# Linear attention: step table, predicated merge of block levels, a gate chain in two steps

## Chip, core and metric

One Trainium2 chip, of which the kernel uses one core. The time is device microseconds of one execution. Every time below is in microseconds unless it says ns. The engines are named as the profile names them: PE is TensorE's matmul, PEld its weight load, DVE is VectorE, ACT is ScalarE, POOL is GpSimd, SP is SyncE, which issues the weight transfers.

## What is computed

Two blocks in float32 on a sequence of 256 positions with 1024 channels. The first is a hybrid layer (attention with forgetting, a short convolution, a gated delta rule, a gated feed-forward part with a convolution, and a gated embedding `ple`). The second block has two layers; the mixer of its second one is a gated linear attention, the part that most of the change is about:

```python
def _gla_mixer(h, w_in, w_gk_up, b_gk, norm_gain, w_out):
    proj = h @ w_in
    q, k, v, g_out, gk_low = jnp.split(proj, [...], axis=-1)
    log_a = jax.nn.log_sigmoid(gk_low @ w_gk_up + b_gk) / GLA_GATE_TEMP
    ...
    b = jnp.cumsum(gi, axis=2)
    o_inter = jnp.einsum('bhlk,bhkv->bhlv', qi * jnp.exp(b), state)
    diff = b[:, :, :, None, :] - b[:, :, None, :, :]
    decay = jnp.exp(jnp.where(causal[:, :, None], diff, -jnp.inf))
    attn = jnp.einsum('bhijk,bhjk->bhij', qi[:, :, :, None, :] * decay, ki)
    o_intra = jnp.einsum('bhij,bhjv->bhiv', attn, vi)
    ...
    o = _rmsnorm(o, norm_gain) * silu(g_out)
    return o @ w_out
```

There are 4 heads, with 128 key channels and 256 value channels each.

## The kernel before

**Units.** Every large product is cut into units of 1 MB of weights (128 partitions x 2048 columns, float32). SP loads a unit into one of 5 buffers (`raw`, L742) when the unit five before it is done. A float32 product is made of three passes over a high part and a low part: ACT copies the unit rounded to fp32r into `whi` (L865, `split_high`, 3 buffers, so it waits until the unit three before is done), DVE writes the difference into `low` (L1241, `split_low`), and PE multiplies high by high, high by low and low by high (L1874 to L1876 for units of kind C, which fill one bank of PSUM, 4 or 5 in turn; L1891 to L1893 for kind D, which accumulate over four units into banks 0 to 3; L1860 to L1864 for a C unit that starts right behind a normalisation).

**Order.** One list, `order`, is written at build time, and each engine takes from it, in that order, the part it has in every step; each engine works its own instructions strictly in turn and waits on semaphores. `("mm", u, 0)` and `("mm", u, 1)` are the two halves of unit u on PE. At half 0 of unit u ACT makes the high part of unit u + 2, at half 1 DVE makes the low part of unit u + 2. In the front part and in the first mixer of the second block, steps are placed by a table of half units. In linear attention `weave` spreads them by weights: a list of steps, each with an amount of unit halves that goes in front of it.

**Linear attention** has 12 units of `gla_w_in`: four C units for q and k (124 to 127), four D units for v (128 to 131), four C units for the output gate (132 to 135). Then four D units of `gla_w_out` (136 to 139). Between them stand:
- `norm_wide` (PE L1914) spreads the norm's reciprocal over PSUM, and DVE copies it (L1297). `gla_low` (PE L2167 to L2169) makes the gate's 16 channels. `gla_qk` (DVE L1302, `scaled`) takes q and k from PSUM, which frees the C unit's bank.
- the gate chain, `gla_gate`: PE L2176 and L2177, DVE L1730 and L1731, ACT's Exp and Ln (L1130, L1132, each behind a table load), and DVE's subtraction L1733. All of DVE's part is one step, so DVE waits for ACT in the middle of it. `gla_cum` (PE L2186, ACT L1137) sums over positions.
- eight levels of blocks of 1, 2, 4 ... 128 positions. Level l has `gla_arg` (DVE L1770, L1771: exponents), ACT's Exp (L1146), `gla_mul` (DVE L1777, L1778: q and k times it, into one buffer `Cl`), `gla_pairs(l + 1)` (PE L2208: 8 products into banks 6 and 7) and `gla_mask(l + 1)`, which takes them out of PSUM: level 0 by L1750 times the identity into `attn`, levels 1 to 4 by L1750 times a 0/1 matrix `lev` into a second buffer `atmp` and L1752, `attn + atmp`; levels 5 to 8 by copies of blocks (L1745, L1738).
- `gla_values` (PE L2219, L2220), `gla_sum` (ACT's sums of squares L858 and Sqrt L1036, DVE L1252 and L1584), `gla_g` (DVE L1302, ACT's Silu L1158), and `gla_turn` (PE transposes L2233, DVE L1790, ACT L1168, DVE L1797), which makes the input of `gla_w_out`.

**The norm** at the end of each part (`last_product`): the last unit's result is added to x in three pieces (DVE L1632 or L1630), PE transposes x (L1907), ACT takes the high part of each pair of tiles (L896), DVE its low part (L1281, `("norm", i, pair)`), and DVE makes one more unit's low part (`split_late`). Norm 2 is the one in front of `w_ple_gate`, whose first units are 75, 76 and 77.

Of the kernel before, what the change touches and what calls it, by code (L numbers as in the profile page):

```python
# [22 lines left out]
def build(nc, a):  # L23

    T, D = a["x"].shape[1:]
# [460 lines left out]
    fill = []
    for i in range(4):
        u = unit_d(w_gla, 256 * i, "h", 2 * i, i == 0, i == 3, h_ready, c0=2 * GK)
        fill.append((u, ("gla_v", u)) if i == 3 else (u,))
    for e in range(2):  # L490
        u = unit_c(w_gla, 2 * GK + D + 256 * e, "h", h_ready)
        fill.append((u, ("gla_g", e, u)))
    mixed = [(2, ("gla_pairs", 0))]
    for l in range(8):
        fill_by = (1.8, 1.2) if l < 5 else (1, 0.8)
        mixed += [(0, ("gla_arg", l)), (fill_by[0], ("gla_mask", l)), (0, ("gla_mul", l)),
                  (fill_by[1], ("gla_pairs", l + 1))]
    weave(fill, mixed + [(0.5, ("gla_mask", 8))])
    fill = []
    for e in range(2, D // 256):  # L500
        u = unit_c(w_gla, 2 * GK + D + 256 * e, "h", h_ready)
        fill.append((u, ("gla_g", e, u)))
# [1777 lines left out]
```

## Time and profile before

| what | us |
|---|---|
| median of 3 runs | 1202.05 |
| lowest and highest of them | 1201.32, 1202.52 |
| the profiled execution, its own time | 1200.95 |
| span of its instructions | 1199.2 |

The profile is one execution. Its own time is its span and 1.75 us around it. PE is busy in 95% of the span, the other engines in 64% (DVE), 46% (ACT) and 4% (POOL). The chain of work that ended last is 77% PE, 14% DVE and 4% ACT. The section on rows below shows, for two stretches of the span, the timeline (one line for an instruction or a run of like ones) and the waits: a wait is time in which an engine stood idle in front of an instruction, with the instruction that released it. The granted clock is 1.00 at 2.4 GHz and 0.50 at 1.2 GHz.

### The profile page before, as it was taken

What the parts mean: (1) busy time and instruction counts of PE and PEld (TensorE: products, weight loads), DVE (VectorE), ACT (ScalarE), POOL (GpSimd) and SP (SyncE); (2) the same over time, 40 slices, a digit from 0 to 9 for tenths busy, and PEclk for the clock granted to TensorE, in tenths of its full rate; (3) what the DMA queues carried; (4) which work ended last, traced back from release to release, by engine and by line L of the source; (5) the groups of instructions that cost most, each with busy time, mean ns of one, the idle gap of its engine ahead of it and who ended that gap; (6) DMA issues with size and microseconds to landing.
All of it is one profiled execution on the core that took longest, in us unless ns stands there. A gap on an engine that the chain in (4) does not pass through costs nothing.

```text
span 1199.2 us, 17834 instructions
## 1 busy us (share of the span) xinstructions
PE 1139.3 (95%) x7630; PEld 1034.0 (86%) x7630; DVE 772.3 (64%) x918; ACT 550.6 (46%) x637; POOL 45.1 (4%) x108
## 2 busy tenths in 40 slices
PE   6989998999999999999998999999989999999996
PEld 6888887898889999997787799999878888999995
DVE  4585777564467988887677564554566856555554
ACT  5466554223445443345555444444443454444443
POOL 8000000000000000000004100000000000000000
PEclk9998999999999999999999999999999999999999
DMA  7765864355355555554453455655533335556551
GB/s 244 201 160 77 132 144 106 63 115 105 107 185 177 177 183 196 184 179 172 141 186 108 141 177 183 200 180 184 183 125 105 106 105 159 193 176 191 196 175 53
DMA packets 128448, 185.08 MB, mean 154 GB/s; under 512 B 6868, under 2 KB 104161, under 8 KB 128370
## 3 DMA queue, kind: packets, MB, share of 16 engines
q1 hardware_dynamic: 123136, 182.46, 51.6%
q10 hardware_dynamic: 4690, 1.36, 0.5%
q8 instruction: 60, 0.98, 0.3%
q0 software_dynamic: 544, 0.13, 0.1%
q14 instruction: 18, 0.15, 0.0%
HBM read 182.89 MB, written 1.05 MB: 153 GB/s over the span
## 4 chain that ended last, share of the span: by engine, by line
PE 77%; DVE 14%; ACT 4%; issue 3%; DMA 1%; ACTq 0%; SPq 0%; DVEq 0%
PE ps L1874 12%; PE ps L1875 12%; PE ps L1876 12%; PE ps L1891 10%; PE ps L1892 10%; PE ps L1893 10%; DVE low L1241 4%; ACT whi L865 1%; PE ps L2078 1%; PE ps L1907 1%; PE ps L2208 1%; PE ps L2084 1%; PE ps L2087 1%; DMA raw<-in_w_in 1%; DVE hlo L1281 1%
## 5 line engine op out<-in xcount | busy, mean ns | idle before, releaser
L865 ACT ACTIVATE whi<-raw 128x2048 fp32r<-128x2048 f32 x172 | 327.9, 1911 | 348.1 <-PE ps L1876 168.0
L1241 DVE TENSOR_TENSOR low<-raw,whi 128x2048 fp32r<-128x2048 f32 x172 | 393.4, 2289 | 56.9 <-ACT whi L865 54.0
L1874 PE MATMUL ps<-hhi,whi 128*128 128x256 f32 x1424 | 410.0, 288 | 10.4 <-DVE arena L1302 5.0
L1875 PE MATMUL ps<-hlo,whi 128*128 128x256 f32 x1424 | 405.2, 285 | 0.0
L1876 PE MATMUL ps<-hhi,low 128*128 128x256 f32 x1424 | 405.1, 284 | 0.0
L1874 PEld LDWEIGHTS ps<-hhi,whi 128*128 128x128 f32 x1424 | 275.2, 193 | 17.0 <-DVE low L1241 10.2
L1875 PEld LDWEIGHTS ps<-hlo,whi 128*128 128x128 f32 x1424 | 275.2, 193 | 1.7 <-issue 0.2
L1876 PEld LDWEIGHTS ps<-hhi,low 128*128 128x128 f32 x1424 | 275.1, 193 | 0.0
L1891 PE MATMUL ps<-whi,ahi 128*128 128x512 f32 x416 | 164.7, 396 | 8.4 <-issue 4.6
L1892 PE MATMUL ps<-low,ahi 128*128 128x512 f32 x416 | 162.8, 391 | 0.0
L1893 PE MATMUL ps<-whi,alo 128*128 128x512 f32 x416 | 162.5, 391 | 0.0
L1891 PEld LDWEIGHTS ps<-whi,ahi 128*128 128x128 f32 x416 | 78.6, 189 | 25.1 <-issue 8.7
L1893 PEld LDWEIGHTS ps<-whi,alo 128*128 128x128 f32 x416 | 78.4, 188 | 17.0
L1892 PEld LDWEIGHTS ps<-low,ahi 128*128 128x128 f32 x416 | 78.7, 189 | 14.6
L1719 DVE TENSOR_TENSOR cy<-cy 128x512 f32<-128x512 f32 x32 | 22.1, 692 | 75.4 <-ACT cy L1118 75.4
L1724 DVE TENSOR_TENSOR alo<-cy,ahi 128x512 fp32r<-128x512 f32 x32 | 22.2, 692 | 72.8 <-ACT ahi L1126 72.8
L1891 PE MATMUL ps<-whi,hhi 128*128 128x512 f32 x160 | 64.4, 402 | 4.6 <-DVE hlo L1281 2.7
L1892 PE MATMUL ps<-low,hhi 128*128 128x512 f32 x160 | 63.0, 394 | 0.0
L1893 PE MATMUL ps<-whi,hlo 128*128 128x512 f32 x160 | 63.0, 394 | 0.0
L1891 PEld LDWEIGHTS ps<-whi,hhi 128*128 128x128 f32 x160 | 30.4, 190 | 11.5 <-DVE low L1241 5.2
L1408 DVE SCALAR_TENSOR_TENSOR cy<-conv,colp,cy 128x256 f32<-128x256 f32 x88 | 38.8, 482 | 1.6
L1893 PEld LDWEIGHTS ps<-whi,hlo 128*128 128x128 f32 x160 | 30.5, 190 | 6.6
(381 smaller groups left out, 1199.7 us busy)
## 6 DMA issues: line engine op xcount, KB each, us to landing
raw<-in_ffn_w SPq DMA_DIRECT2D x64, 1024.0 KB, 5.2
raw<-in_w_in SPq DMA_DIRECT2D x32, 1024.0 KB, 10.3
raw<-in_w_up SPq DMA_DIRECT2D x22, 1024.0 KB, 5.1
raw<-in_gla_w_in SPq DMA_DIRECT2D x12, 1024.0 KB, 5.2
raw<-in_w_down SPq DMA_DIRECT2D x11, 1024.0 KB, 4.9
raw<-in_ab_w_in SPq DMA_DIRECT2D x8, 1024.0 KB, 5.2
raw<-in_w_branch SPq DMA_DIRECT2D x6, 1024.0 KB, 6.0
raw<-in_w_o SPq DMA_DIRECT2D x4, 1024.0 KB, 4.7
```

Source lines behind the costliest of these rows:

```text
L865: act.activation(whi[:, u % SPLIT, :], raw[:, u % RAW, :], ACT.Copy).then_inc(sem("hi_done"), 1)
L1241: dve.tensor_tensor(wlo[:, u % RAW, :], raw[:, u % RAW, :], whi[:, u % SPLIT, :].bitcast(F32), ALU.subtract).then_inc(sem("lo_done"), 1)
L1281: dve.scalar_tensor_tensor(out=hlo[:, k, :], in0=ps[:, turn_banks[i][pair], (k % 2) * T:(k % 2 + 1) * T], scalar=gain(i, k), in1=hhi[:, k, ...
L1408: ins = dve.scalar_tensor_tensor(out=out[:, q, :], in0=src, scalar=w, in1=out[:, q, :], op0=ALU.mult, op1=ALU.add)
L1719: own(dve.tensor_tensor(y, y, y, ALU.mult), "relu2_sq", i + 1)
L1724: dve.tensor_tensor(alo[:, s, :], cy[:, i % 2, :, :], ahi[:, s, :].bitcast(F32), ALU.subtract)\
L1874: pe.matmul(out, wh, hi[:, k0 + k, :], start=k == 0, stop=False)
L1875: pe.matmul(out, wh, lo[:, k0 + k, :], start=False, stop=False)
L1876: ins = pe.matmul(out, wl, hi[:, k0 + k, :], start=False, stop=k == nk - 1)
L1891: pe.matmul(out, xh, wh, start=start, stop=False)
L1892: pe.matmul(out, xh, wl, start=False, stop=False)
L1893: ins = pe.matmul(out, xl, wh, start=False, stop=stop)
```

## The change

1. In `last_product`, for norm 2 alone, `split_late` moves from behind all four pairs to between pair 1 and pair 2.
2. In linear attention, the units and the steps between them are placed by a table of half units in place of `weave`. D units of v wait for the gate's part of DVE (`gla_abs`) as well.
3. `gla_gate` on DVE is two steps, `gla_gate` and `gla_decay`, with other steps between them.
4. `gla_mask` of levels 1 to 4 is one `copy_predicated` from PSUM into `attn`, under the mask `lev`; `atmp` is gone.
5. The waits of `gla_arg(0)` for q and k move to `gla_mul(0)`; the other `gla_mul` wait until PE has read `Cl` of the level before.

```diff
-        for pair in range(1, 4):
-            step("norm", i, pair)
-        step("split_late", u)
+        step("norm", i, 1)
+        if i == 2:
+            step("split_late", u)
+        step("norm", i, 2)
+        step("norm", i, 3)
+        if i != 2:
+            step("split_late", u)
...
-    weave(fill, [(3, ("norm_wide", 5)), (0, ("gla_low",)), (1, ("gla_gate",)), (4, ("gla_cum",))])
...
+        u = unit_d(w_gla, 256 * i, "h", 2 * i, i == 0, i == 3, h_ready + [("gla_abs", 1)], c0=2 * GK)
...
+    steps_at = {
+        1: [("norm_wide", 5), ("gla_low",)],
+        3: [("gla_gate",)],
...
+        17: [("gla_arg", 6), ("gla_mul", 6), ("gla_mask", 6)],
...
+    for at, (u, *then) in enumerate(linear):
+        order.append(("mm", u, 0))
+        flush()
+        for s in steps_at.get(2 * at, ()):
+            step(*s)
+        order.append(("mm", u, 1))
+        held.extend(then)
+        for s in steps_at.get(2 * at + 1, ()):
+            step(*s)
...
                 dve.scalar_tensor_tensor(out=gla, in0=gmin, scalar=-2.0, in1=two, op0=ALU.mult, op1=ALU.add).then_inc(sem("gla_abs"), 1)
+
+            def gla_decay():
                 dve.wait_ge(sem("gla_ln"), 2)
                 own(dve.tensor_tensor(gla, gmin, gla, ALU.subtract), "gla_la", 1)
...
-                mask = ident[:, :] if l == 0 else lev[:, l - 1, :]
-                dst = attn if l == 0 else atmp
-                own(dve.tensor_tensor(dst, two, wide(mask.unsqueeze(1), [TT * GH, P]), ALU.mult), "gla_took", l + 1)
-                if l:
-                    link(dve.tensor_tensor(attn, attn, atmp, ALU.add))
+                if l == 0:
+                    own(dve.tensor_tensor(attn, two, wide(ident[:, :].unsqueeze(1), [TT * GH, P]), ALU.mult), "gla_took", 1)
+                    return
+                mask = lev[:, l - 1, :].bitcast(mybir.dt.uint32)
+                own(dve.copy_predicated(attn, wide(mask.unsqueeze(1), [TT * GH, P]), two), "gla_took", l + 1)
...
                 if l == 0:
                     dve.wait_ge(sem("gla_b"), 2)
-                    dve.wait_ge(*gla_qk_ready[0])
-                    dve.wait_ge(*gla_qk_ready[1])
...
                 dve.wait_ge(sem("gla_E"), l + 1)
+                if l == 0:
+                    dve.wait_ge(*gla_qk_ready[0])
+                    dve.wait_ge(*gla_qk_ready[1])
+                else:
+                    dve.wait_ge(sem("gla_paired"), 2 * l + 2)
```

How instructions stand in a row, at three places. The line numbers of the changed kernel are other than those of before: its L1669 is L1632 of before, L1318 is L1281, L1278 is L1241, L1326 to L1351 are L1289 to L1314, L1767 and L1768 are L1730 and L1731, L1772 is L1733, L1807 and L1808 are L1770 and L1771, L1788 is L1750, L1819 and L1820 are L1777 and L1778.

**DVE at norm 2.** The rows are the additions to x, the low parts of the norm's tiles (`hlo`) and the low part of unit 76 (`low`). Before:

```order
L1632 TENSOR_TENSOR xres<-xres,ps 128x1024
L1632 TENSOR_TENSOR xres<-xres,ps 128x512
L1281 SCALAR_TENSOR_TENSOR hlo<-ps,colp,hhi 128x256 x2
L1632 TENSOR_TENSOR xres<-xres,ps 128x512
L1281 SCALAR_TENSOR_TENSOR hlo<-ps,colp,hhi 128x256 x6
L1241 TENSOR_TENSOR low<-raw,whi 128x2048
L1289 RECIPROCAL rs<-rs 128x2
```

Changed:

```order
L1669 TENSOR_TENSOR xres<-xres,ps 128x1024
L1669 TENSOR_TENSOR xres<-xres,ps 128x512
L1318 SCALAR_TENSOR_TENSOR hlo<-ps,colp,hhi 128x256 x2
L1669 TENSOR_TENSOR xres<-xres,ps 128x512
L1318 SCALAR_TENSOR_TENSOR hlo<-ps,colp,hhi 128x256 x2
L1278 TENSOR_TENSOR low<-raw,whi 128x2048
L1318 SCALAR_TENSOR_TENSOR hlo<-ps,colp,hhi 128x256 x4
L1326 RECIPROCAL rs<-rs 128x2
```

The low part of unit 76 moved in front of the last four low parts of the norm.

**DVE from the start of linear attention to its first exponents.** `low` rows are units 126, 127, 128 and on; L1302 (L1339) is `gla_qk`; L1730, L1731 and L1733 (L1767, L1768 and L1772) the gate. Before:

```order
L1241 TENSOR_TENSOR low<-raw,whi 128x2048
L1297 COPY arena<-ps 128x256
L1302 SCALAR_TENSOR_TENSOR arena<-ps,arena 128x512
L1314 TENSOR_TENSOR arena<-ps,arena 16x256
L1241 TENSOR_TENSOR low<-raw,whi 128x2048
L1730 TENSOR_SCALAR arena<-ps 128x1024
L1731 SCALAR_TENSOR_TENSOR arena<-arena,ps 128x1024
L1733 TENSOR_TENSOR arena<-arena 128x1024
L1241 TENSOR_TENSOR low<-raw,whi 128x2048
L1302 SCALAR_TENSOR_TENSOR arena<-ps,arena 128x512
L1241 TENSOR_TENSOR low<-raw,whi 128x2048
L1302 SCALAR_TENSOR_TENSOR arena<-ps,arena 128x512 x2
```

Changed:

```order
L1278 TENSOR_TENSOR low<-raw,whi 128x2048
L1334 COPY arena<-ps 128x256
L1351 TENSOR_TENSOR arena<-ps,arena 16x256
L1339 SCALAR_TENSOR_TENSOR arena<-ps,arena 128x512
L1278 TENSOR_TENSOR low<-raw,whi 128x2048
L1767 TENSOR_SCALAR arena<-ps 128x1024
L1768 SCALAR_TENSOR_TENSOR arena<-arena,ps 128x1024
L1339 SCALAR_TENSOR_TENSOR arena<-ps,arena 128x512
L1772 TENSOR_TENSOR arena<-arena 128x1024
L1278 TENSOR_TENSOR low<-raw,whi 128x2048
L1807 TENSOR_TENSOR arena<-arena 128x512
L1808 TENSOR_TENSOR arena<-arena 128x512
```

`gla_qk` of unit 125 moved from behind the gate's subtraction and a low part to in front of both, and the first exponents now come before `gla_qk` of units 126 and 127. On PE, `norm_wide` and `gla_low` moved from behind the first half of unit 125 to in front of it, and `gla_cum` from behind unit 127 to in front of it.

**DVE at levels 0 to 2.** Before:

```order
L1750 TENSOR_TENSOR arena<-ps,ident 128x1024
L1777 TENSOR_TENSOR arena<-arena 128x512
L1778 TENSOR_TENSOR arena<-arena 128x512
L1241 TENSOR_TENSOR low<-raw,whi 128x2048
L1770 TENSOR_TENSOR arena<-arena 128x256x2
L1771 TENSOR_TENSOR arena<-arena 128x256x2
L1750 TENSOR_TENSOR arena<-ps,lev 128x1024
L1752 TENSOR_TENSOR arena<-arena 128x1024
L1777 TENSOR_TENSOR arena<-arena 128x256x2
L1778 TENSOR_TENSOR arena<-arena 128x256x2
```

Changed:

```order
L1788 TENSOR_TENSOR arena<-ps,ident 128x1024
L1819 TENSOR_TENSOR arena<-arena 128x512
L1820 TENSOR_TENSOR arena<-arena 128x512
L1807 TENSOR_TENSOR arena<-arena 128x256x2
L1808 TENSOR_TENSOR arena<-arena 128x256x2
L1278 TENSOR_TENSOR low<-raw,whi 128x2048
L1791 COPY_PREDICATED arena<-lev,ps 128x1024
L1819 TENSOR_TENSOR arena<-arena 128x256x2
L1820 TENSOR_TENSOR arena<-arena 128x256x2
```

The unit's low part moved behind the exponents of level 1, and the pair of instructions that merged a level is one.

## Rows read from the trace of the kernel before

**Rows 1.** The page's first part: busy us, share, instructions of each engine.
```profile
PE 1139.3 (95%) x7630; PEld 1034.0 (86%) x7630; DVE 772.3 (64%) x918; ACT 550.6 (46%) x637; POOL 45.1 (4%) x108
```

**Rows 2.** Waits of PE, 860 to 1000: waiting line, releaser, total, times, longest.
```profile
PE ps L1874 <- DVE arena L1302: 5.0, 1, 5.0
PE ps L2208 <- DVE arena L1778: 4.8, 3, 2.6
PE ps L1891 <- issue: 2.8, 1, 2.8
PE ps L1874 <- DVE low L1241: 0.2, 1, 0.2
```

**Rows 3.** Timeline at norm 2: start, duration, engine, line, idle before it and releaser.
```profile
549.50 1.92 ACT L865 ACTIVATE whi<-raw 128x2048 fp32r<-128x2048 f32 x1
...
561.58 1.66 DVE L1281 SCALAR_TENSOR_TENSOR hlo<-ps,colp,hhi 128x256 fp32r<-128x256 f32 x4 [2.49 <-ACT hhi L896]
...
565.50 0.50 PE L1891 MATMUL ps<-whi,hhi 128*128 128x512 f32 x1 [1.83 <-DVE low L1241]
...
568.01 4.49 DVE L1241 TENSOR_TENSOR low<-raw,whi 128x2048 fp32r<-128x2048 f32 x2 [1.71 <-ACT whi L865]
...
572.67 0.39 PE L1891 MATMUL ps<-whi,hhi 128*128 128x512 f32 x1
```

**Rows 4.** Stretches: length, busy of PE, PEld, DVE, ACT, POOL, granted clock, DMA.
```profile
567.00:570.00 3.00, 3.00 (x8) 2.34 (x7) 1.99 (x1) 2.71 (x2) 0.00 (x0) 0.50 0.43 146
652.50:654.50 2.00, 1.97 (x14) 1.61 (x14) 0.87 (x2) 0.83 (x3) 1.85 (x3) 1.00 0.98 330
897.00:901.00 4.00, 4.00 (x19) 4.00 (x20) 2.77 (x2) 0.00 (x0) 0.00 (x0) 0.50 0.00 0
```

**Rows 5.** Timeline of PE, one wait in the first mixer.
```profile
652.48 0.44 PE L1996 MATMUL ps<-ident,arena 128*128 128x128 f32 x2 [2.03 <-DVE arena L1470]
```

**Rows 6.** Timeline, from the last matmul of unit 124 to `gla_cum`.
```profile
872.68 0.28 PE L1864 MATMUL ps<-hhi,low 128*128 128x256 f32 x1
...
873.27 0.48 DVE L1292 TENSOR_SCALAR cy<-ident,rs 128x128 f32<-128x128 f32 x2
...
882.36 1.12 PE L2176 MATMUL ps<-arena,ones 1*128 1x512 f32 x2
...
886.10 1.23 DVE L1730 TENSOR_SCALAR arena<-ps 128x1024 f32<-128x1024 f32 x1 [3.83 <-PE ps L2177]
...
892.08 1.23 DVE L1733 TENSOR_TENSOR arena<-arena 128x1024 f32<-128x1024 f32 x1 [3.50 <-ACT arena L1132]
...
896.99 0.55 PE L1874 MATMUL ps<-hhi,whi 128*128 128x256 f32 x1 [4.98 <-DVE arena L1302]
...
904.79 1.95 PE L2186 MATMUL ps<-tri,arena 128*128 128x128 f32 x16
```

**Rows 7.** Timeline, a table load of ACT and the activation behind it.
```profile
909.20 1.28 ACT L1146 ACT_TABLE_LOAD   x1
...
910.49 1.06 ACT L1146 ACTIVATE arena<-arena 128x1024 f32<-128x1024 f32 x1
```

**Rows 8.** Timeline, mask and multiplication of a level, and a wait of PE for one.
```profile
917.51 1.23 DVE L1750 TENSOR_TENSOR arena<-ps,lev 128x1024 f32<-128x1024 f32 x1
...
918.77 1.23 DVE L1752 TENSOR_TENSOR arena<-arena 128x1024 f32<-128x1024 f32 x1
...
920.03 0.69 DVE L1777 TENSOR_TENSOR arena<-arena 128x512 f32<-128x512 f32 x1
...
928.76 3.67 PE L2208 MATMUL ps<-arena 128*128 128x128 f32 x16 [2.59 <-DVE arena L1778]
```

**Rows 9.** Timeline, the turn of the result and the first product of `gla_w_out`.
```profile
980.50 2.29 DVE L1790 SCALAR_TENSOR_TENSOR arena<-ps,colp,arena 128x128 f32<-128x128 f32 x8 [1.36 <-issue]
...
983.62 0.77 PE L1891 MATMUL ps<-whi,ahi 128*128 128x512 f32 x1 [2.78 <-issue]
...
987.92 1.03 PE L2233 MATMUL ps<-ident,arena 128*128 128x128 f32 x8
```

More of the change, by code:

```diff
@@ L480, in build, with gla_qk @@
     w_gla = a["gla_w_in_2"][0]
-    fill = []
-    for e in range(2 * GK // 256):
+    linear, v_first = [], {}
+    def gla_qk(e):
         u = unit_c(w_gla, 256 * e, "h", h_ready)
-        fill.append((u, ("gla_qk", e, u)))
-    weave(fill, [(3, ("norm_wide", 5)), (0, ("gla_low",)), (1, ("gla_gate",)), (4, ("gla_cum",))])
[L486 to L489, printed above, removed]
@@ L490, in build @@
-    for e in range(2):
-        u = unit_c(w_gla, 2 * GK + D + 256 * e, "h", h_ready)
[L492 to L502, printed above, removed]
@@ L503, in build, with gla_v, gla_g @@
-    weave(fill, [(0, ("gla_values", 0)), (0, ("gla_sum", 0)), (0.5, ("gla_values", 1)), (1, ("gla_sum", 1)),
-                 (1, ("gla_turn", 0))])
+        linear.append((u, ("gla_qk", e, u)))
+    def gla_v(i):
+        u = unit_d(w_gla, 256 * i, "h", 2 * i, i == 0, i == 3, h_ready + [("gla_abs", 1)], c0=2 * GK)
+        v_first.setdefault("u", u)
+        linear.append((u, ("gla_v", u)) if i == 3 else (u,))
+    def gla_g(e):
+        u = unit_c(w_gla, 2 * GK + D + 256 * e, "h", h_ready)
+        linear.append((u, ("gla_g", e, u)))
@@ new lines, in build @@
+    gla_qk(0)
+    gla_qk(1)
+    gla_qk(2)
+    gla_qk(3)
+    gla_v(0)
+    gla_v(1)
+    gla_v(2)
+    gla_v(3)
+    gla_g(0)
+    gla_g(1)
+    gla_g(2)
+    gla_g(3)
+    steps_at = {
+        1: [("norm_wide", 5), ("gla_low",)],
+        3: [("gla_gate",)],
+        4: [("gla_decay",)],
+        5: [("gla_cum",), ("gla_arg", 0)],
+        8: [("gla_pairs", 0), ("gla_mask", 0), ("gla_mul", 0), ("gla_arg", 1)],
+        9: [("gla_pairs", 1), ("gla_mask", 1)],
+        10: [("gla_mul", 1), ("gla_arg", 2), ("gla_pairs", 2), ("gla_mask", 2), ("gla_mul", 2), ("gla_arg", 3)],
+        11: [("gla_pairs", 3), ("gla_mask", 3)],
+        12: [("gla_mul", 3)],
+        14: [("gla_arg", 4), ("gla_pairs", 4)],
+        15: [("gla_mask", 4), ("gla_mul", 4), ("gla_pairs", 5), ("gla_arg", 5)],
+        16: [("gla_mask", 5), ("gla_mul", 5), ("gla_pairs", 6)],
+        17: [("gla_arg", 6), ("gla_mul", 6), ("gla_mask", 6)],
+        19: [("gla_pairs", 7), ("gla_arg", 7), ("gla_mask", 7)],
+        20: [("gla_mul", 7), ("gla_pairs", 8), ("gla_mask", 8), ("gla_values", 0), ("gla_sum", 0), ("gla_values", 1)],
+        21: [("gla_sum", 1)],
+        22: [("gla_turn", 0)],
+    }
@@ L505, in build @@
+    for at, (u, *then) in enumerate(linear):
[7 more added lines that the diff above has]
+            step(*s)
+    flush()
+    for s in steps_at.get(2 * len(linear), ()):
+        step(*s)
     us = [unit_d(a["gla_w_out_2"][0], 256 * i, "a", 2 * i, i == 0, i == 3, [("gla_lo", 1 + 2 * (i // 2))])
@@ L655, in build @@
         attn = view(5120, 1024).rearrange("p (g i) -> p g i", g=TT * GH)
-        atmp = view(6144, 1024).rearrange("p (g i) -> p g i", g=TT * GH)
         across = by(view(7168, 512), GH)
@@ L1809, in _ @@
                          ple_p=ple_p, ple_x=ple_x, lam=lam, pool_mm=pool_mm,
-                         relu2=relu2, gla_gate=gla_gate, gla_mask=gla_mask, gla_mul=gla_mul,
+                         relu2=relu2, gla_gate=gla_gate, gla_decay=gla_decay, gla_mask=gla_mask, gla_mul=gla_mul,
                          gla_arg=gla_arg,
@@ L2238, in _ @@
             gla_qk_ready = [took(s[2]) for s in order if s[0] == "gla_qk"][2:]
-            v0 = [s[1] for s in order if s[0] == "gla_v"][0] - 3
+            v0 = v_first["u"]
             gla_v_ready = [(sem(g), v + 1) for g, v in units[v0]["free"]]
```

## The prediction

> **What bounds the kernel now.** I read the page first: PE is busy in 95% of the span, DVE in 64% [rows 1]. So an edit pays only where it takes away a wait of PE or a stretch at the low clock, and the reader should look for those two. Next come the waits of PE in linear attention [rows 2]: 0.2 for a low part in front of unit 125, 5.0 in front of unit 127 (its bank is freed by `gla_qk`, L1302, which stands on DVE behind the gate's subtraction), 4.8 in three waits for `gla_mul` (L1778), and 2.8 in front of `gla_w_out`. Together 12.8. Third, the granted clock: behind the wait of 4.98 it was 0.50 from 897 to 901 at least [rows 4], so half of 4 us, 2.0, was lost. Behind the wait of 2.59 sixteen matmuls of 128x128 took 3.67 [rows 8] where the sixteen of `gla_cum` took 1.95 [rows 6]: 1.7 lost. At `gla_w_out`, twelve matmuls took 987.92 - 983.62 = 4.30 [rows 9]; unit 76, with twenty-four, took 572.67 - 565.50 = 7.17, with one stretch at 0.50 that spans 567 to 570 [rows 3, 4]. Taking 1.7 lost there, 24 cost 5.5 and 12 cost 2.7, so 1.6 was lost at `gla_w_out`. Clock in linear attention: 2.0 + 1.7 + 1.6 = 5.3. What can be won there at most is 12.8 + 5.3 = 18.1.
>
> **Norm 2.** Before, unit 75 ends at 565.50 - 1.83 = 563.67, and PE waits 1.83 for the low part of unit 76, which DVE makes last. Its high part was ready at 549.50 + 1.92 = 551.4, and DVE stood idle for 2.49 until 561.58 [rows 3]. Moved into that gap it runs from 559.1 for 2.25 (half of the 4.49 that two took) and ends at 561.3, 0.2 before the norm's next high part comes, so nothing behind it is late. PE starts unit 76 at 563.7 at full clock and ends it at 569.2. What is late next is the low part of unit 77: DVE starts it at 568.01, behind the norm's sums on ACT, which are not moved, and ends it at 570.3 [rows 3]. PE then waits 1.1. Unit 77 starts at 570.3 in place of 572.67: **2.4 won**. What follows is paced by PE.
>
> **Gate chain.** I walk the new order with the durations of the trace, from the end of unit 124 (872.8). PE now has `norm_wide` next, which needs DVE's diagonals, ready at 873.27 + 0.48 = 873.75 [rows 6]: a new wait of 1.0 where 0.25 was. `norm_wide` and `gla_low` (3.2), unit 125 (5.9) and the gate's products (3.6; DVE takes them up 3.74 after 882.36 [rows 6]) bring DVE's gate to 886.7. Its two instructions end at 889.2, ACT's Exp and Ln 3.4 later (892.08 less the 2.5 of DVE from 886.10 [rows 6]), at 892.6, DVE's subtraction at 893.9. Meanwhile DVE frees unit 125's bank, at no cost in the pause that was 3.50 idle [rows 6], and PE does unit 126 from 886.6 to 892.5. So PE waits **1.4** for `gla_cum`, where it waited 4.98 before, and unit 127 stands behind it, ready. `gla_cum` costs the 1.7 it did (its 1.95 overlaps the next), moved and not added. The D units' new wait for `gla_abs` is met 12 us before it is reached. On DVE, the first exponents now wait for ACT's sums of `gla_cum` (896.5); queued behind them are `gla_qk` of 126 and 127 and the low part of 129. They end at 904.1, and `gla_pairs(0)` wants the last at 904.3.
>
> **Levels.** DVE is the second bound here. Before, each of levels 1 to 4 has two instructions of 1.23, 1.26 from start to start [rows 8], between PE's products and the next multiplication. The trace has no `copy_predicated`. Bounds from the nearest rows: half an instruction of L1750, 0.6, if no pass over a second operand costs anything; and the pair it replaces, 2.5. I take 1.23, that of L1750, because it too reads 1024 columns of PSUM against `lev` and writes as many. So 4 x 1.26 = 5.0 leave DVE; none of that is PE's by itself. The Trainium skill (VectorE: DVE Perf Modes, "Why PSUM operands drop a tier") holds a float32 instruction with an operand in PSUM to one element per cycle; by an estimate from the page's table that would be some 1.2, which leaves the sum as it is and speaks against the 0.6.
>
> Walk: `gla_pairs(0)` ends at 906.0; DVE has mask 0, multiplication 0 (1.35) and exponents 1 (1.3) until 910.0, then unit 130's low part (2.25), mask 1 (1.25), multiplication 1 until 914.9. PE has the second half of unit 128, pairs 1 and the first half of 129, until 913.4. So PE waits **1.5** for multiplication 1, since a low part stands in front of mask 1. Then, by the same steps, each time DVE's last instruction against the moment at which PE is free for it: pairs 3, 919.4 against 919.5; pairs 4, 925.5 against 929.7; pairs 5, 934.1 against 934.2; pairs 6, 938.7 against 939.0; pairs 7, 945.6 against 949.5; pairs 8, 954.1 against 954.2. The added waits of `gla_mul` for `gla_paired` hold nothing: behind each stands only DVE's own next mask or low part, and PE's products end before (level 6 is the one case where the multiplication now runs ahead of the mask). At the end, the values run 5.2 from 955.2, one half of unit 134 having gone in front of them; the sums and scalings end at 965.4 against 966.2, and `gla_turn(0)` now has half of unit 135 behind it. Its DVE and ACT part took 3.1 (980.50 to the 983.62 at which PE goes on [rows 9]); half a C unit takes 2.9. Start 966.9, done 970.0, PE free at 970.0: the wait of 2.78 is gone, and so is its slow stretch.
>
> So six handovers have 0.0 to 0.3 to spare. My walk leaves out small gaps between kinds of work on both engines, so some of these will be late by tenths: I take 0.6 for all.
>
> **Two more table loads** on ACT, since Silu of unit 132 now comes before the last Exp. A load is 1.28, and the activation starts right behind it, 909.20 + 1.28 against 910.49 [rows 7]. By the walk Silu ends at 947.6 and the load at 948.9, DVE's argument for Exp comes at 949.2: hidden, with 0.3 to spare there and 2 more before DVE comes to multiplication 7 (it still takes mask 7 and `gla_g` in between).
>
> **Sum.** Linear attention: 12.8 waited + 5.3 of clock - (1.0 + 1.4 + 1.5) of new waits = 14.2, less 0.6: 13.6. With norm 2, 16.0. The profiled execution took 1200.95 (span 1199.2), so it would take 1185.0; the median of the runs is 1.1 above it, so 1202.05 - 16.0 = **1186.0**.
>
> **Rivals.**
> *The new waits bring the clock down.* For it: at norm 2 a wait of 1.83 was followed by 0.50 [rows 3, 4]. Against: one of 2.03 left it at 1.00 [rows 4, 5], and the two shorter ones of L2208 (4.8 less 2.6 [rows 2]) did as well. The new ones are 1.0, 1.4, 1.5 and, at norm 2, 1.1. Each stretch costs 1.7: with one 1187.7, with two 1189.4.
> *`copy_predicated` takes 2.5, as much as the pair.* Then 1.25 more in masks 1, 2 and 4, which have nothing to spare (mask 3 has 4): 1.2 + 1.1 + 1.1, and a wait of 2.7 with a slow stretch behind it, 1.7: 1186.0 + 5.1 = 1191.1. It works on one more stream than a plain copy; no row here shows that a stream costs.
> *The table doesn't hold.* Six tight handovers in a row, in queues that can't overtake: if DVE is a microsecond behind my walk at 904 (a high part that comes late on ACT, which now has three splits between exponentials), each level inherits it: 4 to 8 lost, 1190 to 1194.
> *Slower.* The mask of levels 1, 2 and 4 stands between PE's products and the next multiplication. Each microsecond above 1.23 in `copy_predicated` costs 3, and up to three waits become long enough for a slow stretch, 5 in all. The 16.0 are gone when 3x + 5 = 16, at x = 3.7: above 4.9 for one, twice the pair it replaces, the kernel is slower; at 6, by 3, 1205. Nothing on DVE of 1024 columns in the trace is near that.
> *A switch of tables costs more than the load.* If an activation came 1.4 later behind each load, the Sqrt of the sums would end later and the last scaling at 966.8 against 966.2: 0.7 more, 1186.7. The Trainium skill (ScalarE: Activation LUTs, "What ACT_TABLE_LOAD costs") has 1.28 for the load and about 1.38 of drain with it. By that rule the walk would go so; the trace disagrees, the activation starts 1.29 after its load [rows 7].
>
> **Chances.** The walk holds (1184.5 to 1188): 0.60. One or two slow stretches, the dear copy, or a few late handovers (1188 to 1191.5): 0.22. The table doesn't hold (1191.5 to 1199): 0.07. The dearer switch of tables (1186.7): 0.02. More won than walked, to 1183, where the new waits come out smaller or the copy is 0.6: 0.04. No change: 0.02. Slower: 0.03. The range, 1183.5 to 1191.5, takes in both bounds of the copy. What a measurement of this kernel can tell from no change is 0.2%, 2.4: faster 0.95, same 0.02, slower 0.03.
>
> **What the new profile would show.** Right: no wait of 1.83 at norm 2 but one of about 1.1 for unit 77's low part; in linear attention waits of PE of about 1.0, 1.4 and 1.5 and none above 2; the granted clock at 1.00 from 872 to 990; `copy_predicated` at 1.2; `gla_w_out` some 14 earlier. Wrong: a wait for `gla_mul` above 2 with 0.50 behind it, a `copy_predicated` near 2.5, or a wait in front of units 129 to 131 for a low part, which would say that ACT's splits, queued behind exponentials, set the pace.

## The result, and the profile after

| | before | changed |
|---|---|---|
| median | 1201.74 (4 runs, 1201.32 to 1202.52) | 1183.66 (4 runs, 1182.57 to 1184.53) |
| profiled execution, its span | 1200.95, 1199.2 | 1182.57, 1180.8 |

The ratio is 0.9858, with a 95% interval of 0.9843 to 0.9874: 18.1 faster, where 16.0 was forecast. The median lies inside the range, 0.2 above its low end, and 0.8 below the part of it that the walk had to itself (1184.5 to 1188).

The page's first part, beside [rows 1]: PE lost 6 of its busy time with as many instructions, since less of the span is at the low clock: by the trace's record of the clock 30.7 us at 0.50 before and 13.7 changed, without the last microseconds, which are at 0.50 in both. DVE lost 4 with the four sums that went.

```profile
PE 1133.2 (96%) x7630; PEld 1029.1 (87%) x7630; DVE 768.0 (65%) x914; ACT 553.0 (47%) x639; POOL 45.2 (4%) x108
```

The waits of PE from 855 to 985, which answer to [rows 2] (line, releaser, total, times, longest). Of 12.8 in six waits, 2.2 in two are left. The wait of 2.8 at `gla_w_out`, `issue` in [rows 2], is gone altogether.

```profile
PE ps L2250 <- DVE arena L1820: 1.4, 1, 1.4
PE ps L1956 <- DVE cy L1329: 0.8, 1, 0.8
```

Norm 2, the timeline beside [rows 3] (start, length, engine and line, operation, out<-in, idle time before it and its releaser). The low part of unit 76 runs at 557.20, in the pause; the norm's next low parts start 0.27 behind ACT's high part and are not late; unit 77 waits 1.25 for its low part. 1.1 was forecast.

```profile
557.20 2.28 DVE L1278 TENSOR_TENSOR low<-raw,whi 128x2048 fp32r<-128x2048 f32 x1
559.76 1.66 DVE L1318 SCALAR_TENSOR_TENSOR hlo<-ps,colp,hhi 128x256 fp32r<-128x256 f32 x4 [0.27 <-ACT hhi L933]
...
568.54 0.50 PE L1933 MATMUL ps<-whi,hhi 128*128 128x512 f32 x1 [1.25 <-DVE low L1278]
```

Linear attention, the timeline beside [rows 6, 8, 9]: `norm_wide`, the gate on DVE, its subtraction, `gla_cum`, the first `copy_predicated`, the wait for multiplication 1, DVE's turn, and `gla_turn(1)` on PE. `gla_cum` starts within 0.1 of the end of the subtraction, and PE did not wait: it was in unit 126 until then.

```profile
869.71 0.49 PE L1956 MATMUL ps<-cy,ones 128*128 128x128 f32 x2 [0.83 <-DVE cy L1329]
...
882.61 1.23 DVE L1767 TENSOR_SCALAR arena<-ps 128x1024 f32<-128x1024 f32 x1 [5.98 <-PE ps L2219]
...
888.66 1.22 DVE L1772 TENSOR_TENSOR arena<-arena 128x1024 f32<-128x1024 f32 x1 [2.97 <-ACT arena L1169]
...
889.94 2.05 PE L2228 MATMUL ps<-tri,arena 128*128 128x128 f32 x16
...
908.51 1.30 DVE L1791 COPY_PREDICATED arena<-lev,ps 128x1024 f32<-128x1024 uint32 x1
...
911.20 2.05 PE L2250 MATMUL ps<-arena 128*128 128x128 f32 x16 [1.40 <-DVE arena L1820]
...
963.57 2.29 DVE L1832 SCALAR_TENSOR_TENSOR arena<-ps,colp,arena 128x128 f32<-128x128 f32 x8 [0.85 <-DVE arena L1339]
...
969.53 1.03 PE L2275 MATMUL ps<-ident,arena 128*128 128x128 f32 x8
```

Why unit 126 lasted longer: the stretches of the changed kernel (length, busy of PE, PEld, DVE, ACT, POOL, granted clock, DMA). Right behind the gate's products the clock is at 0.51, with no wait of PE in front of it; from 890 to 960 it is at 1.00.

```profile
883.00:886.00 3.00, 3.00 (x17) 3.00 (x16) 2.66 (x3) 0.87 (x1) 0.00 (x0) 0.51 0.07 29
869.00:882.00 13.00, 12.29 (x84) 9.93 (x84) 6.55 (x9) 4.34 (x3) 0.00 (x0) 1.00 0.39 124
890.00:960.00 70.00, 68.52 (x466) 62.43 (x466) 53.22 (x59) 38.32 (x47) 0.00 (x0) 1.00 0.37 121
```

**Where the time went.** I cut each profile at three instructions that all kernels have: the first low part of norm 2 (L1281 of before), the diagonals of norm 5 (L1292) and `gla_turn(1)` on PE (L2233, its second run). Norm 2's edit lies in the second piece, linear attention in the third; the first is the same program in all.

| us | front | norm 2 to 5 | attention | rest |
|---|---|---|---|---|
| before | 556.8 | 316.4 | 114.65 | 211.3 |
| changed | 555.0 | 314.1 | 100.4 | 211.3 |
| difference | 1.8 | 2.3 | 14.3 | 0.0 |

The front's 1.8 is not the change's: the program is the same there, and the clock was at 0.50 for 13.7 us of it before and for 10.2 changed, which at half speed is 1.7.

### The profile page after: what moved, and what is told of

Read it like the earlier page. It is cut to its first block, busy times and chain, and to the rows that moved or that the text cites. A ratio compares the mean times of both kernels' runs of the same rounds, so it can differ in the third digit from the quotient of the medians.

```text
span 1180.8 us, 17834 instructions
## 1 busy us (share of the span) xinstructions
PE 1133.2 (96%) x7630; PEld 1029.1 (87%) x7630; DVE 768.0 (65%) x914; ACT 553.0 (47%) x639; POOL 45.2 (4%) x108
## 4 chain that ended last, share of the span: by engine, by line
PE 80%; DVE 12%; ACT 4%; issue 3%; DMA 1%; ACTq 0%; SPq 0%; DVEq 0%
PE ps L1916 13%; PE ps L1917 13%; PE ps L1918 13%; PE ps L1933 10%; PE ps L1934 10%; PE ps L1935 10%; DVE low L1278 4%; ACT whi L902 1%; PE ps L2250 1%; PE ps L1949 1%; PE ps L2120 1%; PE ps L2126 1%; PE ps L2129 1%; DMA raw<-in_w_in 1%; PE ps L1902 1%
## 5 line engine op out<-in xcount | busy, mean ns | idle before, releaser
L1278 DVE TENSOR_TENSOR low<-raw,whi 128x2048 fp32r<-128x2048 f32 x172 | 394.2, 2295 | 51.8 <-ACT whi L902 48.8
L1934 PEld LDWEIGHTS ps<-low,ahi 128*128 128x128 f32 x416 | 78.3, 188 | 14.4
```

The lines of the kernel that those rows point to most:

```text
L1278: dve.tensor_tensor(wlo[:, u % RAW, :], raw[:, u % RAW, :], whi[:, u % SPLIT, :].bitcast(F32), ALU.subtract).then_inc(sem("lo_done"), 1)
L1934: pe.matmul(out, xh, wl, start=False, stop=False)
```

## Experiments

The four pieces of every profile of the study, by the same cuts. The three kernels with a bias row come at the end.

| us | front | norm 2 to 5 | attention | rest | PE's waits for `gla_mul` |
|---|---|---|---|---|---|
| changed, again | 556.5 | 314.2 | 100.3 | 211.3 | 1.4 |
| e1, norm 2 alone | 557.6 | 314.25 | 114.15 | 211.3 | 4.8 |
| e2, all but norm 2 | 557.6 | 317.2 | 100.3 | 211.3 | 1.4 |
| e3, two masks | 558.1 | 314.3 | 107.3 | 211.3 | 5.3 |
| e4, gate in one step | 556.55 | 314.3 | 100.3 | 211.3 | 1.4 |
| e5, copy alone | 559.9 | 314.9 | 109.7 | 211.3 | 2.0 |
| e6, copy twice | 556.9 | 314.25 | 105.5 | 211.3 | 6.6 |
| e7, low part early | 559.6 | 314.2 | 98.96 | 211.3 | none |
| e11, table alone | 556.3 | 314.8 | 107.2 | 211.3 | 5.3 |
| e9, bias as a row | 557.6 | 317.5 | 98.7 | 211.3 | 1.4 |
| e10, three edits | 556.8 | 317.4 | 96.6 | 211.3 | none |
| e12, memsets moved | 557.1 | 314.3 | 96.6 | 211.3 | none |

The front moves by 5 with one and the same program, so a median says less than the third piece, which repeats to 0.1 (100.4, 100.3, 100.3).

A profile shows one execution. The mean granted clock is on record for all of them, so what the low clock took, (1 - mean clock) x span, can be averaged; a stretch of 3.4 at 0.50 counts 1.7. The clock is on record to 0.001, which is 1.2 us of one execution. Means in us:

| | executions | time | low clock | the rest |
|---|---|---|---|---|
| before, beside changed again, e1, e2 and e7 | 17 | 1201.9 | 18.4 | 1183.5 |
| changed, again | 4 | 1183.6 | 10.3 | 1173.3 |
| e1, norm 2 alone | 12 | 1198.6 | 15.9 | 1182.7 |
| e2, all but norm 2 | 6 | 1188.5 | 13.8 | 1174.7 |
| before, beside e3 to e6 | 17 | 1200.3 | 17.5 | 1182.8 |
| e3, two masks | 7 | 1191.6 | 14.3 | 1177.3 |
| e4, gate in one step | 4 | 1184.3 | 10.9 | 1173.3 |
| e6, copy twice | 5 | 1192.5 | 14.5 | 1178.0 |
| e10, three edits | 5 | 1184.7 | 12.5 | 1172.2 |
| e12, memsets moved | 5 | 1180.8 | 9.2 | 1171.6 |

A ± behind a difference of these means is twice its standard error.

**The changed kernel again.**

> The changed kernel once more, to see how much of 18.1 is the change's. Theory A (the two profiles differ by 2.4 at norm 2 and 14.3 in linear attention; the 1.8 before norm 2 is where stretches at the low clock happened to fall): 16.7 less than before, 1185.0. Theory B (all of 18.1 belongs to the change): 1183.6. In the profile: waits of PE of about 0.8 and 1.4 in linear attention in both.

Measured: 1184.15 (4 runs, 1181.18 to 1184.99) against 1202.55 (17 runs, 1198.13 to 1205.79), ratio 0.9853, interval 0.9829 to 0.9877. The medians say 18.4, nearer to B; the profile has 2.2 at norm 2 and 14.3 in attention, and 0.4 in front, 16.9 in all, which is nearer to A. The interval runs from 14.8 to 20.6 and holds both. By the means the gain is 8.0 ± 2.4 of low clock and 10.3 ± 0.9 of the rest; norm 2 and attention in the two profiles have 6.8 and 9.8, within these errors.

**Norm 2 alone**, on the kernel before.

```diff
-        for pair in range(1, 4):
-            step("norm", i, pair)
-        step("split_late", u)
+        step("norm", i, 1)
+        if i == 2:
+            step("split_late", u)
+        step("norm", i, 2)
+        step("norm", i, 3)
+        if i != 2:
+            step("split_late", u)
```

> The kernel before with only the low part of unit 76 moved at norm 2. The walk: the wait of 1.83 and the stretch at 0.50 behind it go, a wait of 1.2 for unit 77 comes, 2.4 less: 1199.3. Rival (the new wait brings the clock down as the old one did): 0.7 less, 1201.0.

Measured: 1197.92, ratio 0.9973, interval 0.9957 to 0.9989, which is 1.3 to 5.2 faster. The wait is 1.3, and the stretch behind it is at full clock:

```profile
564.00:571.00 7.00, 5.86 (x26) 4.46 (x24) 2.40 (x3) 6.94 (x8) 0.00 (x0) 1.00 0.48 152
```

The mechanism holds. The rival, a clock that falls behind the new wait, is out: in the ten profiles with this edit no stretch at 0.50 starts there. By the means the edit gives 3.3 ± 1.7, of which 2.5 ± 1.2 is low clock.

**All but norm 2.**

```diff
-        step("norm", i, 1)
-        if i == 2:
-            step("split_late", u)
-        step("norm", i, 2)
-        step("norm", i, 3)
-        if i != 2:
-            step("split_late", u)
+        for pair in range(1, 4):
+            step("norm", i, pair)
+        step("split_late", u)
```

> The changed kernel with norm 2 as before. Theory A: 14.3 less than the kernel before, 1187.4. Theory B (the gain outside norm 2 is 15.7): 1186.0. Norm 2 shows its wait of 1.83 again.

Measured: 1188.22, ratio 0.9894, interval 0.9871 to 0.9917. That is 14.3 below the kernel before, which is A's; B's 15.7 lies just outside the interval (10.0 to 15.5). Attention takes 100.3, as in the changed kernel, so norm 2 and attention don't touch each other. The wait of 1.83 is back, but here the clock stays at 1.00 behind it:

```profile
566.29 0.50 PE L1929 MATMUL ps<-whi,hhi 128*128 128x512 f32 x1 [1.83 <-DVE low L1274]
```

```profile
564.00:571.00 7.00, 5.17 (x24) 3.94 (x23) 4.59 (x4) 6.46 (x8) 0.00 (x0) 1.00 0.48 150
```

This is what the forecast of norm 2 had missed. Of four profiles with norm 2 as before (before, e2, e5, e11) only the first has a stretch at 0.50 behind that wait. In e5 and e11 the second piece is 314.8 and 314.9 against 314.2 with the edit: 0.6 is the edit's certain part (1.83 less 1.25), and 1.7 more comes where the clock would have fallen. The 317.2 of e2 comes from another place: a stretch at 0.50 of 6.8 from 653 on, behind a wait of 2.02:

```profile
651.64 0.44 PE L2034 MATMUL ps<-ident,arena 128*128 128x128 f32 x2 [2.02 <-DVE arena L1503]
```

```profile
653.50:660.00 6.50, 4.89 (x14) 3.65 (x13) 2.21 (x4) 3.81 (x11) 3.77 (x9) 0.50 0.14 48
```

Four profiles are few, and the means say more for the edit than they do: e2 takes 4.9 ± 2.7 more than the changed kernel, 3.5 ± 2.6 of it low clock, and e1 had 2.5 ± 1.2. One stretch of 3.4 in one profile of four would be 0.4. So without the edit more low clock is there in the mean; at which places it falls isn't shown.

**Two masks**: the changed kernel with the old pair.

```diff
-                mask = lev[:, l - 1, :].bitcast(mybir.dt.uint32)
-                own(dve.copy_predicated(attn, wide(mask.unsqueeze(1), [TT * GH, P]), two), "gla_took", l + 1)
+                mask = lev[:, l - 1, :]
+                own(dve.tensor_tensor(atmp, two, wide(mask.unsqueeze(1), [TT * GH, P]), ALU.mult), "gla_took", l + 1)
+                link(dve.tensor_tensor(attn, attn, atmp, ALU.add))
```

> The changed kernel with levels 1 to 4 merged by two instructions again (product with lev into a second buffer, then the sum). 2.48 in place of 1.34 on DVE for each level. Theory P (masks 1, 2 and 4 stand on PE's path in the new table, mask 3 has 4 to spare): the wait at pairs 2 grows from 1.4 to 2.5, new ones of about 1 come at pairs 3 and 5, and a stretch at 0.50 may follow: 3.3 to 5 more than the changed kernel. Rival Q (PE is the bound, DVE's time in the masks is covered): 0 to 0.5 more.

Measured: 1191.68, and attention takes 107.3 in place of 100.3, 7.0 more. P in kind, and more than P in size. The three waits, at pairs 2, 3 and 5:

```profile
915.61 2.95 PE L2252 MATMUL ps<-arena 128*128 128x128 f32 x16 [2.58 <-DVE arena L1822]
...
922.53 2.05 PE L2252 MATMUL ps<-arena 128*128 128x128 f32 x16 [0.54 <-DVE arena L1822]
...
939.49 2.95 PE L2252 MATMUL ps<-arena 128*128 128x128 f32 x16 [2.18 <-DVE arena L1822]
```

They sum to 5.3, 3.9 more than 1.4, and the first and the last are each followed by a stretch at 0.50 (from 916.5 and 940.4, 3.4 long, 1.7 each): 3.9 + 3.4 = 7.3, beside the 7.0 measured. The means agree: 7.4 ± 2.2 above e4 on the same chip, 3.3 ± 3.2 of it low clock. The wait at pairs 5 grew by 2.2, where I had 1: the level 3 pair, which I had called covered, is late too when it meets level 4.

**The copy twice.**

```diff
+                link(dve.copy_predicated(attn, wide(mask.unsqueeze(1), [TT * GH, P]), two))
                 own(dve.copy_predicated(attn, wide(mask.unsqueeze(1), [TT * GH, P]), two), "gla_took", l + 1)
```

> The changed kernel with every copy_predicated done twice (same result). 1.34 more on DVE in each of levels 1 to 4. By the prediction's price of a dearer copy (each us costs 3, since masks 1, 2 and 4 have nothing to spare and mask 3 has 4): 4.0 more than the changed kernel, 5.7 with a stretch at 0.50. Rival (covered): under 1.

Measured: 1192.27; attention 105.5, 5.2 more. The waits at the same three places:

```profile
914.50 2.05 PE L2251 MATMUL ps<-arena 128*128 128x128 f32 x16 [2.75 <-DVE arena L1821]
...
920.70 2.05 PE L2251 MATMUL ps<-arena 128*128 128x128 f32 x16 [1.38 <-DVE arena L1821]
...
937.98 2.05 PE L2251 MATMUL ps<-arena 128*128 128x128 f32 x16 [2.49 <-DVE arena L1821]
```

6.6, which is 5.2 more than 1.4, and no stretch at 0.50 behind any of them in this profile. The mean of its five executions is 8.2 ± 2.3 above that of e4, 3.6 ± 2.9 of it low clock, so some of them had more of it than this one. With 1.34 more in each of four masks, 5.2 is 3.9 for each us, the clock not counted. All four levels are on PE's path, and the price in the forecast, 3, was one level short.

**The copy alone**, in the old order.

```diff
-                mask = ident[:, :] if l == 0 else lev[:, l - 1, :]
-                dst = attn if l == 0 else atmp
-                own(dve.tensor_tensor(dst, two, wide(mask.unsqueeze(1), [TT * GH, P]), ALU.mult), "gla_took", l + 1)
-                if l:
-                    link(dve.tensor_tensor(attn, attn, atmp, ALU.add))
+                if l == 0:
+                    own(dve.tensor_tensor(attn, two, wide(ident[:, :].unsqueeze(1), [TT * GH, P]), ALU.mult), "gla_took", 1)
+                    return
+                mask = lev[:, l - 1, :].bitcast(mybir.dt.uint32)
+                own(dve.copy_predicated(attn, wide(mask.unsqueeze(1), [TT * GH, P]), two), "gla_took", l + 1)
```

> The kernel before, its order unchanged, with copy_predicated for levels 1 to 4. Theory P (in the order of before DVE sets the pace of the levels): the wait of 2.59 shrinks to 0.5 and its stretch at 0.50 goes, those of 1.27 and 0.94 shrink to 0.7 and 0.9; 5.0 less than before, 1196.7. Rival Q (the order sets it, the merge alone is worth little): 0 to 1 less.

Measured: 1195.69, ratio 0.9966 (interval 0.9949 to 0.9984); attention 109.7 against 114.65: 4.95, as P said. Some 0.5 of it is not the copy's: here, as in e1, the clock fell right behind the gate's products and the wait for `gla_qk` was 3.5, where the profile of before had 4.98 and a stretch of 6.8 across it. Against the 114.15 of e1 the copy gives 4.45, which is the 2.8 less of waits below and one stretch, 1.7. Its waits: 4.8 for `gla_mul` became 2.0 in three of at most 0.9.

```profile
PE ps L1873 <- DVE arena L1301: 3.5, 1, 3.5
PE ps L1890 <- issue: 2.8, 1, 2.8
PE ps L2207 <- DVE arena L1777: 2.0, 3, 0.9
PE ps L1873 <- DVE low L1240: 0.2, 1, 0.2
```

**The gate in one step**, in the new table.

```diff
-
-            def gla_decay():
                 dve.wait_ge(sem("gla_ln"), 2)
...
-        4: [("gla_decay",)],
```

> The changed kernel with DVE's part of the gate in one step again, the table as it is. Theory P (what removed the wait of 4.98 is that gla_cum stands in front of unit 127, whose bank is then freed in time even if gla_qk waits behind the subtraction): 0.0 to 0.3 more than the changed kernel. Rival Q (the split into two steps removed it): a wait of some 5 comes back, with a stretch at 0.50, 4 to 7 more.

Measured: 1184.31; attention 100.3, the same. No wait came back:

```profile
PE ps L2247 <- DVE arena L1817: 1.4, 1, 1.4
PE ps L1953 <- DVE cy L1328: 0.8, 1, 0.8
```

So the two steps are worth nothing here. What removed the wait of 4.98 is the table, by this order: between the gate and `gla_cum` PE has a unit whose bank is free, and unit 127, whose bank waits for DVE, comes behind `gla_cum`.

**The table alone**: two masks, one step, norm 2 as before (the diffs of e2, e3 and e4 together).

> The new table alone: two instructions for a level's merge, the gate in one step, norm 2 as before. From the stretch between the norm's diagonals and gla_turn(1), 114.6 before, 100.3 changed, 107.4 with the table and two instructions, 109.7 with the old order and the copy. Theory (the two-step gate is worth nothing): 107.4, as with two steps. Rival: the one-step gate costs 5 here, 112.

Measured: 107.2 in attention (one execution, 1191.39). The parts of attention, from 114.65: the table alone 7.4, the copy alone 4.95, both 14.3. Together they give 2.0 more than their sum (2.5, if the 114.15 of e1 is taken for before). In the old order the copy takes away 2.8 of waits and one stretch at 0.50; in the table it takes away 3.9 and two stretches, those from 915.1 and 939.0 behind the waits of 2.60 and 2.17, which are in this profile as they are in e3. The 2.78 at `gla_w_out` is there in both profiles with the old order (e1, e5) and in none with the table.

**Unit 130's low part early.**

```diff
-        8: [("gla_pairs", 0), ("gla_mask", 0), ("gla_mul", 0), ("gla_arg", 1)],
+        8: [("gla_pairs", 0), ("split_late", linear[4][0]), ("gla_mask", 0), ("gla_mul", 0), ("gla_arg", 1)],
...
+    late.add(linear[4][0])
```

> The changed kernel with DVE's low part of unit 130 in front of mask 0 in place of behind exponents 1. In the changed kernel's trace DVE stands idle for 2.53 in front of mask 0, and the high part is ready 2.6 before it. The walk: it fits into that pause, mask 1 starts 2.2 earlier, the wait of 1.4 for multiplication 1 goes and no other comes in its place: 1.4 less than the changed kernel. Rival (DVE is the bound of the levels, so that the wait comes back at pairs 3 or 5): 0 to 0.5 less.

Measured: 1181.73 against 1184.15 for the changed kernel on the same chip; attention 98.96, 1.35 less. (The ratios to the kernel before, 0.9842 and 0.9853, have overlapping intervals, so the piece is what carries this.) DVE's low part fills the pause, mask 0 starts 2.43 behind it, and the wait for `gla_mul` is gone without another:

```profile
904.54 2.29 DVE L1279 TENSOR_TENSOR low<-raw,whi 128x2048 fp32r<-128x2048 f32 x1
906.97 1.23 DVE L1789 TENSOR_TENSOR arena<-ps,ident 128x1024 f32<-128x1024 f32 x1
```

**The bias as a row** of the gate's product (33 rows, of which 17 carry data and the others are multiplied by zero).

```diff
-        wgu = view(14592, GK)[0:GR, :]
-        bgk = view(9216, GK)[0:1, :]
+        GX = 33
+        wgu = view(14592, GK)[0:GX, :]
...
-                    pe.matmul(ps[:, t, :], ones[0:1, :], bgk[:, :], start=True, stop=False)
-                    pe.matmul(ps[:, t, :], gkT[0:GR, t * P:(t + 1) * P], wgu[:, :], start=False, stop=True)\
+                    pe.matmul(ps[:, t, :], gkT[0:GX, t * P:(t + 1) * P], wgu[:, :], start=True, stop=True)\
...
             def lam():
+                dve.memset(gkT[0:GX, :], 1.0).then_inc(sem("gate_rows"), 1)
+                dve.memset(wgu[0:GX, :], 0.0).then_inc(sem("gate_rows"), 1)
+                dve.wait_ge(sem("gate_rows"), 2)
```

> The changed kernel with the gate's bias as a 33rd row of the gate's product (17 rows carry data), so that the two products of one row go: PE's gate is 1.8 in place of 3.6, the chain to gla_cum starts 1.8 earlier. Every profile of this study but the first has a stretch at 0.50 within 1 us behind the gate's products. Theory (it comes from the products with few rows): with half of them it goes, PE then waits 1.4 for gla_cum. Rival (it comes whatever they are): it stays, no wait. Either way 1.8 less from the diagonals to gla_turn(1), 98.5.

Measured (one execution, 1186.83): attention 98.7, 1.6 to 1.7 less. The stretch at 0.50 behind the gate is gone, and PE waits for `gla_cum`, 1.42, as the forecast of the change had it:

```profile
884.50:888.00 3.50, 3.50 (x18) 2.12 (x17) 1.15 (x1) 0.00 (x0) 0.00 (x0) 1.00 0.56 158
888.00:892.00 4.00, 4.00 (x35) 4.00 (x34) 1.90 (x3) 2.61 (x3) 0.00 (x0) 1.00 0.31 126
```

```profile
894.18 2.05 PE L2231 MATMUL ps<-tri,arena 128*128 128x128 f32 x16 [1.42 <-DVE arena L1776]
```

But norm 2 to 5 took 317.5, 3.3 more than in the changed kernel.

**Three edits together**: the diffs of e7 and e9, and `norm_wide` and `gla_low` behind the first half of unit 125.

```diff
-        1: [("norm_wide", 5), ("gla_low",)],
...
         order.append(("mm", u, 0))
+        if at == 1:
+            step("norm_wide", 5)
+            step("gla_low")
         flush()
```

> The changed kernel with three edits: unit 130's low part in front of mask 0 (1.4 less), the bias as a row (1.8 less), and norm_wide and gla_low behind the first half of unit 125, as in the kernel before (a wait of 0.25 in place of 0.83, 0.6 less). The walk: 3.8 less than the changed kernel, 96.5 from the diagonals to gla_turn(1) and 0.3 in it from the first edit of order, 1180. Rival (the pauses of DVE that the edits use are the same ones): under 2.

Measured: attention 96.6, as walked, yet the median is 1185.18 (5 runs, 1183.59 to 1185.62), 5 above what was expected, no better than the changed kernel. The loss is in the second piece again, 317.4. My two memsets, put into the step `lam`, stood on DVE in front of `ab_qk`, and the wait of PE there is 1.9 where it was 0.9:

```profile
PE ps L2038 <- DVE arena L1343: 1.9, 1, 1.9
```

That is 0.9 of the 3.2 (1.87 less 0.94); the rest is a stretch at 0.50 of 6.8 from 652 on, as in e9.

**The memsets moved** from `lam` to another step of DVE, `pool_mm`, in front of its wait; the rest as in e10.

```diff
             def lam():
-                dve.memset(gkT[0:GX, :], 1.0).then_inc(sem("gate_rows"), 1)
-                dve.memset(wgu[0:GX, :], 0.0).then_inc(sem("gate_rows"), 1)
-                dve.wait_ge(sem("gate_rows"), 2)
...
+                dve.memset(gkT[0:GX, :], 1.0).then_inc(sem("gate_rows"), 1)
+                dve.memset(wgu[0:GX, :], 0.0).then_inc(sem("gate_rows"), 1)
+                dve.wait_ge(sem("gate_rows"), 2)
```

> The kernel of the three edits, whose two memsets (the constant rows of the gate's product) stood on DVE in front of the first attention scores of the second block: the wait of PE there grew from 0.93 to 1.9, and behind the wait of 2.03 for the values' part 45 us later a stretch at 0.50 of 6.8 began. Here they stand in DVE's idle 2.47 in front of the pool mixer's scaling. Theory: the wait is 0.93 again, the stretch between norm 2 and the diagonals is 314.2 in place of 317.4, that from the diagonals to gla_turn(1) stays at 96.6, and the median is 3 to 4 under the changed kernel's: 1180.5. Rival (the stretch at 0.50 near 652 has nothing to do with the memsets): 316.5 and 1182.5.

Measured: 1180.72 (5 runs, 1178.86 to 1183.74) against 1199.84 for the kernel before on the same chip, ratio 0.9831, interval 0.9805 to 0.9858. The second piece is 314.3, attention 96.6, the wait in front of `ab_qk` 0.9 (the other row is the wait for `gla_cum`), and no stretch at 0.50 near 652:

```profile
PE ps L2234 <- DVE arena L1779: 1.4, 1, 1.4
...
PE ps L2038 <- DVE arena L1343: 0.9, 1, 0.9
```

The 0.9 is shown. That the memsets also brought the stretch near 652 is shown less well: e2 has it without them, though none of the other eleven profiles without them in `lam` does. The means of five executions each, on two chips, are for it: 3.3 ± 1.7 less low clock than e10.

In attention this kernel is 3.7 shorter than the changed one, by profiles; by ratios to the kernel before (0.9831 against 0.9858) it is some 3 faster, but the two intervals overlap.

## Why the prediction was right, point by point

- **Attention.** The sum, 12.8 + 5.3 less the new waits of 3.9, gave 14.2 (13.6 with the 0.6 for late handovers), and the piece shrank by 14.3 in the profile and in its repeat. The waits of 1.0 and 1.5 came as 0.83 and 1.40. The lost clock was 5.5, not 5.3: behind the wait of 4.98 it was at 0.50 until 901.5, 4.5 us and not 4. The wait of 4.98, the 2.78 at `gla_w_out` and the slow stretches behind them went. None of the new waits was followed by a stretch at 0.50, so the rival that priced this (1187.7, 1189.4) did not come; the stretch that did come stood where neither the walk nor a rival had one.
- **The wait of 1.4 for `gla_cum` did not come.** The walk assumed full clock behind the gate's products. There the clock fell for 3.4, which lost 1.7, PE ended unit 126 that much later, and the wait was used up by it: a cost in another place and of nearly the same size. So it is luck that the sum comes within 0.1 of what was measured: with both corrections it is 12.8 + 5.5 - 0.83 - 1.40 - 1.7 = 14.4. e9 shows it: with the stretch gone, the wait is 1.42. The line "the granted clock at 1.00 from 872 to 990" was wrong for that reason.
- **0.6 for late handovers was wrong.** None of the six was late. This is the difference between 16.0 and the 16.6 in norm 2 and attention.
- **Front.** The rest is 1.8 in a part that the change doesn't reach. The profile of before had more stretches at 0.50 there; with one program the front ran from 555.0 to 559.9 in the study. In medians the gain is 18.1 and 18.4, in norm 2 and attention 16.6 in both profiles; whether the change shifts where the clock falls elsewhere is open, since the means (8.0 ± 2.4 of low clock, where these pieces have 6.8) can't tell 1 or 2 us.
- **Norm 2.** 2.4 was forecast and 2.3 measured, but the term mixes two things. 0.6 is there each time, and the 1.7 behind the old wait only in one of four profiles; these alone would make the mean nearer to 1. The means of the executions are nearer to the forecast and above it: 3.3 ± 1.7 in e1 and 4.9 ± 2.7 between e2 and the changed kernel, 2.5 and 3.5 of it low clock. So the size stands, and the place that the forecast gave the lost clock doesn't, in most profiles.
- **`copy_predicated`** took 1.30 to 1.32 (1.23 was taken; the bounds were 0.6 and 2.5). The estimate from the Trainium skill (VectorE: DVE Perf Modes, "Why PSUM operands drop a tier"), 1.2, is borne out to 0.1, and the 0.6 is not.
- **The price of a dearer copy** was mis-sized: 3.9 for each us, not 3, since level 3 is not covered (e3, e6). The rival with the dear copy would have cost 1.25 x 3.9 = 4.9 and more with the clock; e3, with 1.2 more in each level, took 7.0.
- **The gate in two steps.** The walk counted the subtraction in its new place and did not ask what the split itself brings; e4 shows that it was worth 0.0, and that the new order of steps alone had done the work.
- **The table loads** were the smallest rival, and it is out. The timeline of ACT in the changed kernel has a load in front of the last Exp, one in front of a Silu (L1195) and one in front of the Sqrt of the sums:

```profile
944.48 1.28 ACT L1180 ACT_TABLE_LOAD   x1
946.45 0.63 ACT L1180 ACTIVATE arena<-arena 128x512 f32<-128x512 f32 x1 [0.68 <-DVE arena L1801]
...
949.42 1.28 ACT L1195 ACT_TABLE_LOAD   x1
950.71 0.63 ACT L1195 ACTIVATE arena<-arena 128x512 f32<-128x512 f32 x1
...
955.45 1.28 ACT L1073 ACT_TABLE_LOAD   x1
956.74 0.30 ACT L1073 ACTIVATE ss<-ss,eps 128x4 f32<-128x4 f32 x1
```

The 0.68 behind the first is a wait for DVE, so that pair can't show a drain. In the other two the activation starts 1.29 behind the start of its load, as in [rows 7]. By the Trainium skill (ScalarE: Activation LUTs, "What ACT_TABLE_LOAD costs") about 1.38 more would belong to a switch; the trace has none of it.

## What to carry to other kernels

Where in-order queues hand work to each other, walk the new order with the durations of the old trace and write down each handover with the time to spare: this walk had each new wait within 0.2 but one, which a stretch at the low clock hid. Count such a stretch as a term of its own, with the share of profiles in which it is there, and take more than one profile, and the mean clock of all executions, before it is booked as won. A small helper put into a queue costs nothing only if it stands in a pause of that engine: the same two memsets cost 0.9 in one step and nothing in another.
